# Moving the work region and the two halves of x inside SBUF, in a float32r transformer-layer kernel

## The chip, the cores and the metric

The kernel runs on one core of one Trainium2 chip, in a single launch. The metric is device time in microseconds (us) from one execution of the whole program; the figure for a kernel is the median of its runs. The granted TensorE clock of a stretch has two levels, 1.2 and 2.4 GHz; the profile prints them as 0.50 and 1.00, or as a mean between them.

## The reference, cut to what matters

One layer of a diffusion backbone over 512 latent tokens of width 2048, with 256 context tokens that only supply the start state of a scan. All data is float32.

```
h_lat = modulate(rms_norm(x, norm1_gain), sh1, sc1)          # 512 x 2048
h_ctx = modulate(rms_norm(ctx, norm1_gain), csh1, csc1)      # 256 x 2048
mix   = token_mixer(h_lat, h_ctx, w_in, ...)                 # w_in 2048 x 7168: gMLP heads and gated scans
x     = x + g1 * (mix @ w_out)                               # 2048 x 2048
h     = modulate(rms_norm(x, norm2_gain), sh2, sc2)
x     = x + g2 * (square(relu(h @ w_ff1)) @ w_ff2)           # 2048 x 8192, 8192 x 2048
return rms_norm(x, final_gain)
```

The shifts, scales and gates come from a further product, silu(c) @ w_ada (2048 x 12288).

## The kernel before

**Precision.** Every large product is made of three float32r products. A value is split into a high part (the float32r rounding, written by ScalarE) and a low part (the rest, by GpSimd or VectorE), and the kernel adds hi*hi, hi*lo and lo*hi in PSUM. For the latent stream the two halves of x (normalised and modulated, transposed) are `h_hi` and `h_lo`, 16 tiles of 512 columns each; for the context they are `c_hi` and `c_lo`, 16 tiles of 256 columns; for the hidden activations of the MLP they are `hid_hi` and `hid_lo`, 8 tiles of 512 columns.

**Weights.** They arrive as 448 units of 128 x 1024 through four slots `raw` (L247). ScalarE writes `w_hi` (L344), GpSimd writes `w_lo` (L313; VectorE does 32 of them in the context heads, L705), each with two slots. `lo_done` releases TensorE, `unit_used` gives the slots back.

**Two shapes of product.** A *tall* unit (lines 1105 to 1107, and 1392 to 1394 for the first units of the MLP) has 128 weight columns as the stationary operand and a tile of h (or c) as the moving operand. A *wide* unit (lines 1119 to 1121) has it the other way round: 128 columns of h, c or hid are the stationary operand, and 512 columns of weights the moving one. In the names of a matmul row, `bank<-A,B`, A is the moving and B the stationary operand; each matmul has its own weight load, listed as PEld.

**Stages, in order of time.** (1) adaLN product for the first norm: `ada1_w` is the moving operand (L1067). (2) context values, wide with c as the stationary operand, and context heads, tall with c moving. (3) latent values, half wide, half tall. (4) eight scan heads, tall with h moving, with steps of the previous head's scan between the products (L1227 and others) and the second adaLN product on VectorE (L753). (5) gMLP: u tall, v wide. (6) output projection, wide with h as the stationary operand. (7) the MLP in eight blocks: 384 tall matmuls with h moving, then 384 wide matmuls with hid as the stationary operand. Each engine runs a list written by hand, ordered by semaphores; loops over heads and blocks are hardware loops.

**Places in SBUF.** `build` hands out byte offsets within a partition. `fixed` gives the next free offset, rounded up to 32 bytes; `work` gives a place at a number of KB behind `w0`, where tensors of different stages lie over one another. The start is 16512 (the base of 16481, rounded up). So the kernel before has:

| offset (bytes) | what | offset modulo 64 |
|---|---|---|
| 16512 | raw, then w_hi (32896) and w_lo (41088) | 0 |
| 49280 to 114816 | h_hi, h_lo; in stage 1 ada1_w lies over both, and junk over h_hi | 0 |
| 114816 | ident (512 bytes) | 0 |
| 115328 | ones (32 bytes), after it mask and ten more small tensors | 0 for ones, 32 for those after it |
| 118368 to 228960 | work region of 108 KB: c_hi at +0, c_lo at +16 KB; hid_hi at +16 KB (134752), hid_lo at +32 KB (151136); x_tok, x_res, mix, scan buffers | 32 |

All tensors in the work region start at a whole number of KB behind w0, so they keep its remainder. The stationary slices are 512 bytes long and start at multiples of 512 bytes behind their tensor.

Of the kernel before, what the change touches and what calls it, by code (L numbers as in the profile page):

```python
# [28 lines left out]
F32 = mybir.dt.float32  # L29
F32R = mybir.dt.float32r  # L30
# [5 lines left out]
P = 128  # L36
D = 2048
KT = D // P
SEQ, CTX = 512, 256
# [9 lines left out]
KB = 1024  # L49
# [18 lines left out]
def build(nc, ctx_x, x, w_stream, w_ada, cols, small, masks, bs_row, final_row, ws_t, out):  # L68
    with ExitStack() as stack:
        base = nc.sbuf_base  # L70
        top = nc.sbuf_usable_end
        where = [base + (-base) % 32]

        def fixed(name, shape, dt=F32):
            n = 1 if dt == U8 else 4
            for s in shape[1:]:
                n *= s
            t = nc.alloc_sbuf_tensor_at(name, shape, dt, offset=where[0])
            where[0] += n + (-n) % 32
            return t  # L80
# [1 line left out]
        raw = fixed("raw", [P, 4, UNIT])  # L82
        w_hi = fixed("w_hi", [P, 2, UNIT], F32R)
        w_lo = fixed("w_lo", [P, 2, UNIT], F32R)
        r1 = where[0]
        h_hi = fixed("h_hi", [P, KT, SEQ], F32R)
        h_lo = fixed("h_lo", [P, KT, SEQ], F32R)
        ada1_w = nc.alloc_sbuf_tensor_at("ada1_w", [P, 4, 4096], F32, offset=r1)
        junk = nc.alloc_sbuf_tensor_at("junk", [P, D], F32, offset=r1)
        ident = fixed("ident", [P, P])  # L90
        ones = fixed("ones", [P, 8])
        mask = fixed("mask", [P, LEVELS, P], U8)
# [5 lines left out]
        oml = fixed("oml", [P, 2, HEADS])  # L98
        lbt = fixed("lbt", [P, 3, 2 * HEADS])
        stat = fixed("stat", [P, 64])  # L100
        w0 = where[0]
        assert w0 + 108 * KB <= top, (w0, top)

        def work(name, kb, shape, dt=F32):
            return nc.alloc_sbuf_tensor_at(name, shape, dt, offset=w0 + int(kb * KB))
# [6 lines left out]
        VG_COL, OG_COL = col[:, 160:168], col[:, 168:176]  # L112
        lbl = fixed("lbl", [P, 2, 2 * HEADS])
        w0 = where[0]
        assert w0 + 108 * KB <= top, (w0, top)


        c_hi = work("c_hi", 0, [P, KT, CTX], F32R)
# [1386 lines left out]
```

## Time and profile before

| | |
|---|---|
| median of 3 runs | 2747.98 us (2743.83 to 2750.40) |
| span of the profiled execution, first to last instruction | 2748.0 us |
| PE busy | 2638.0 us, 96% of the span |
| PEld, DVE, ACT, POOL busy | 2125.1, 1271.9, 728.3, 1002.8 us |
| mean granted TensorE clock | 0.984 |

The profiled execution's own time, apart from its span, is not given; the span equals the median of the runs to 0.1 us. A matmul's busy time overlaps with that of the next, so busy time doesn't say what a matmul costs. What it costs is the distance from its start to the start of the next, called its pitch here: the time of a stretch without waits divided by the number of matmuls in it.

### The profile page before, as it was taken

To read this page: it belongs to the slowest core of one execution; us is meant where nothing else is said; L and a number is where in the kernel's file an instruction comes from. 1 tells how busy PE (TensorE), PEld (TensorE's weight loads), DVE (VectorE), ACT (ScalarE), POOL (GpSimd) and SP (SyncE) were. 2 spreads that over 40 slices of the span, in tenths; PEclk is the share of its full clock that TensorE was granted. 3 is DMA by queue.
4 is the path that set the end of the run, shared out by engine and by line. 5 is a ranking of instruction groups with operands and counts; after the bars stand their busy time and mean duration, and the time that the engine had idled before them with its cause. 6 is when DMAs were issued, how large, how long until landed. Compare 5 with 4: busy or idle time off the path is not lost.

```text
span 2748.0 us, 33371 instructions
## 1 busy us (share of the span) xinstructions
PE 2638.0 (96%) x12236; PEld 2125.1 (77%) x12236; DVE 1271.9 (46%) x1495; ACT 728.3 (27%) x931; POOL 1002.8 (36%) x420
## 2 busy tenths in 40 slices
PE   8989999999999999998899999999999999999997
PEld 1469887777777887787788888888888888888885
DVE  2386447777888623666423223332332333323324
ACT  1254222222222223223322222212222122221222
POOL 0240243323332343343344444444444444444442
PEclk9999999999999999999999999999999999999998
DMA  9635454433344352364223232222222222222222
GB/s 409 250 115 166 154 193 151 146 132 122 122 137 138 131 214 92 115 232 143 69 93 114 92 99 93 98 93 95 95 92 99 92 99 92 95 96 92 99 92 99
DMA packets 104715, 353.80 MB, mean 129 GB/s; under 512 B 9937, under 2 KB 10193, under 8 KB 100689
## 3 DMA queue, kind: packets, MB, share of 16 engines
q1 hardware_dynamic: 104224, 352.46, 37.3%
q8 instruction: 40, 0.66, 0.1%
q10 hardware_dynamic: 432, 0.54, 0.1%
q14 instruction: 19, 0.15, 0.0%
HBM read 348.77 MB, written 4.19 MB: 128 GB/s over the span
## 4 chain that ended last, share of the span: by engine, by line
PE 58%; issue 28%; POOL 10%; DVE 2%; DMA 1%; ACT 1%; POOLq 0%; SPq 0%; DVEq 0%; ACTq 0%
POOL w_lo L313 10%; PE bank L1105 9%; PE bank L1107 9%; PE bank L1106 9%; PE bank L1119 9%; PE bank L1120 9%; PE bank L1121 9%; PE bank L1067 3%; DMA ada_w<-in_w_ada 1%; DVE prep_tmp L666 0%; DVE x_tok L656 0%; DVE x_res L1056 0%; ACT junk L392 0%; PE bank L1154 0%; PE bank L1092 0%
## 5 line engine op out<-in xcount | busy, mean ns | idle before, releaser
L313 POOL TENSOR_TENSOR w_lo<-raw,w_hi 128x1024 fp32r<-128x1024 f32 x416 | 1002.6, 2410 | 1719.7 <-ACT w_hi L344 1719.7
L344 ACT ACTIVATE w_hi<-raw 128x1024 fp32r<-128x1024 f32 x448 | 475.0, 1061 | 1768.6 <-PE bank L1107 870.3
L1105 PE MATMUL bank<-h_hi,w_hi 128*128 128x512 f32 x1696 | 673.3, 397 | 2.9 <-POOL w_lo L313 2.9
L1107 PE MATMUL bank<-h_hi,w_lo 128*128 128x512 f32 x1696 | 665.0, 392 | 0.0
L1106 PE MATMUL bank<-h_lo,w_hi 128*128 128x512 f32 x1696 | 664.3, 392 | 0.0
L1119 PE MATMUL bank<-w_hi,hid_hi 128*128 128x512 f32 x1024 | 404.9, 395 | 0.0
L1120 PE MATMUL bank<-w_lo,hid_hi 128*128 128x512 f32 x1024 | 404.9, 395 | 0.0
L1121 PE MATMUL bank<-w_hi,hid_lo 128*128 128x512 f32 x1024 | 404.8, 395 | 0.0
L1105 PEld LDWEIGHTS bank<-h_hi,w_hi 128*128 128x128 f32 x1696 | 321.3, 189 | 67.0 <-POOL w_lo L313 3.4
L1107 PEld LDWEIGHTS bank<-h_hi,w_lo 128*128 128x128 f32 x1696 | 320.3, 189 | 67.5
L1106 PEld LDWEIGHTS bank<-h_lo,w_hi 128*128 128x128 f32 x1696 | 321.1, 189 | 64.0
L1025 DVE TENSOR_TENSOR hid_sb<-relu_sb 128x512 f32<-128x512 f32 x64 | 159.5, 2492 | 450.2 <-ACT relu_sb L596 450.2
L753 DVE SCALAR_TENSOR_TENSOR ada_acc<-ada_w,cs,ada_acc 128x512 f32<-128x512 f32 x240 | 268.7, 1120 | 87.0 <-DMA ada_w<-in_w_ada 80.6
L1034 DVE TENSOR_TENSOR g_tmp<-bank,g_row 128x512 f32<-128x512 f32 x128 | 87.5, 684 | 476.5 <-PE bank L1121 476.5
L1121 PEld LDWEIGHTS bank<-w_hi,hid_lo 128*128 128x128 f32 x1024 | 192.1, 188 | 46.8
L1120 PEld LDWEIGHTS bank<-w_lo,hid_hi 128*128 128x128 f32 x1024 | 192.1, 188 | 46.8
L1119 PEld LDWEIGHTS bank<-w_hi,hid_hi 128*128 128x128 f32 x1024 | 192.1, 188 | 46.7
L1119 PE MATMUL bank<-w_hi,h_hi 128*128 128x512 f32 x448 | 178.5, 398 | 13.9 <-POOL w_lo L313 7.3
L1120 PE MATMUL bank<-w_lo,h_hi 128*128 128x512 f32 x448 | 176.3, 394 | 0.0
L1121 PE MATMUL bank<-w_hi,h_lo 128*128 128x512 f32 x448 | 176.3, 394 | 0.0
L1036 DVE TENSOR_TENSOR x_res<-x_res,g_tmp 128x512 f32<-128x512 f32 x128 | 153.3, 1198 | 4.4
L1119 PEld LDWEIGHTS bank<-w_hi,h_hi 128*128 128x128 f32 x448 | 85.4, 191 | 33.1 <-POOL w_lo L313 12.8
(183 smaller groups left out, 2180.9 us busy)
## 6 DMA issues: line engine op xcount, KB each, us to landing
raw<-in_w_stream SPq DMA_DIRECT2D x448, 512.0 KB, 3.5
ada_w<-in_w_ada SPq DMA_DIRECT2D x128, 512.0 KB, 4.1
ada_w<-in_w_ada SPq DMA_DIRECT2D x16, 2048.0 KB, 11.9
x_tok<-in_x SPq DMA_DIRECT2D x4, 1024.0 KB, 16.5
x_res<-in_x SPq DMA_DIRECT2D x4, 1024.0 KB, 11.9
out<-x_res SPq DMA_DIRECT2D x4, 1024.0 KB, 4.0
ctx_tok<-in_ctx_x SPq DMA_DIRECT2D x2, 1024.0 KB, 16.1
fin_row<-in_final_row SPq DMA_DIRECT2D x1, 1024.0 KB, 6.6
```

The costliest lines, as they stand in the source:

```text
L313: pool.tensor_tensor(w_lo[:, r % 2], raw[:, r], w_hi[:, r % 2].bitcast(F32), ALU.subtract).then_inc(lo_done, 1)
L344: act.activation(w_hi[:, r % 2], raw[:, r], ACT.Copy).then_inc(hi_done, 1)
L753: dve.scalar_tensor_tensor(acc[:], w[:, m % 2, t], c, acc[:], ALU.mult, ALU.add).then_inc(ada_summed, 1)
L1025: dve.tensor_tensor(hid_sb[:, t % 2], relu_sb[:, t % 2], relu_sb[:, t % 2], ALU.mult).then_inc(hid_made, 1)
L1034: dve.tensor_tensor(g_tmp[:, n % 2], bank[4 * (1 - c % 2) + t][:], g2_row[:, c * 512:(c + 1) * 512], ALU.mult).then_inc(ff2_tmp, 1)
L1036: dve.tensor_tensor(x_res[:, t, c * 512:(c + 1) * 512], x_res[:, t, c * 512:(c + 1) * 512], g_tmp[:, n % 2], ALU.add).then_inc(ff2_added, 1)
L1105: pe.matmul(dst, wh, hi[:, kt], start=(kt == 0), stop=False)
L1106: pe.matmul(dst, wh, lo[:, kt], start=False, stop=False)
L1107: mm = pe.matmul(dst, wl, hi[:, kt], start=False, stop=(kt == KT - 1))
L1119: pe.matmul(b[:], xh, wh, start=(first and k == 0), stop=False)
L1120: pe.matmul(b[:], xh, wl, start=False, stop=False)
L1121: mm = pe.matmul(b[:], xl, wh, start=False, stop=(last and k == 1))
```

## The change

`fixed` calls are put in another order. All small tensors come directly behind the weight slots; w0 follows them; the 108 KB work region follows w0; behind it come h_hi and h_lo, with ada1_w and junk again lying over them. Sizes, places within the work region, what lies over what, and every instruction's order on its engine and semaphore waits stay as they were; only start offsets are other ones. The weight slots don't move.

```diff
         w_lo = fixed("w_lo", [P, 2, UNIT], F32R)
-        r1 = where[0]
-        h_hi = fixed("h_hi", [P, KT, SEQ], F32R)
-        h_lo = fixed("h_lo", [P, KT, SEQ], F32R)
-        ada1_w = nc.alloc_sbuf_tensor_at("ada1_w", [P, 4, 4096], F32, offset=r1)
-        junk = nc.alloc_sbuf_tensor_at("junk", [P, D], F32, offset=r1)
         ident = fixed("ident", [P, P])
         ones = fixed("ones", [P, 8])
...
         lbl = fixed("lbl", [P, 2, 2 * HEADS])
         w0 = where[0]
-        assert w0 + 108 * KB <= top, (w0, top)
+        r1 = w0 + 108 * KB
+        where[0] = r1
+        h_hi = fixed("h_hi", [P, KT, SEQ], F32R)
+        h_lo = fixed("h_lo", [P, KT, SEQ], F32R)
+        ada1_w = nc.alloc_sbuf_tensor_at("ada1_w", [P, 4, 4096], F32, offset=r1)
+        junk = nc.alloc_sbuf_tensor_at("junk", [P, D], F32, offset=r1)
+        assert where[0] <= top, (where[0], top)
```

The offsets that follow:

| | before | modulo 64 | after | modulo 64 |
|---|---|---|---|---|
| small tensors | 114816 to 118368 | | 49280 to 52832 | each as before |
| work region (w0) | 118368 | 32 | 52832 | 32 |
| c_hi, c_lo | 118368, 134752 | 32 | 52832, 69216 | 32 |
| hid_hi, hid_lo | 134752, 151136 | 32 | 69216, 85600 | 32 |
| h_hi (also ada1_w), h_lo | 49280, 82048 | 0 | 163424, 196192 | 32 |

The partition has 229376 bytes (224 KB); its middle is at 114688.

## Rows read from the trace of the kernel before

**Rows 1.** Page, part 1: busy us, share of the span, instructions of each engine.
```profile
PE 2638.0 (96%) x12236; PEld 2125.1 (77%) x12236; DVE 1271.9 (46%) x1495; ACT 728.3 (27%) x931; POOL 1002.8 (36%) x420
```
**Rows 2.** Windows, busy us and instructions per stretch: output projection, then MLP tall, wide, tall.
```profile
core 0: us, PE busy (x) PEld busy (x) DVE busy (x) ACT busy (x) POOL busy (x), PEclk, DMA share, GB/s
1210.00:1240.00 30.00, 30.00 (x133) 24.82 (x134) 19.55 (x21) 8.60 (x14) 13.95 (x6) 1.00 0.81 277
1500.00:1570.00 70.00, 70.00 (x311) 57.97 (x310) 19.10 (x12) 19.93 (x25) 31.11 (x13) 1.00 0.29 93
1590.00:1660.00 70.00, 70.00 (x302) 56.29 (x301) 22.03 (x24) 13.37 (x13) 28.91 (x13) 1.00 0.30 97
1680.00:1750.00 70.00, 70.00 (x311) 57.97 (x310) 20.79 (x13) 20.97 (x26) 30.85 (x13) 1.00 0.29 97
```
**Rows 3.** One line's matmuls within 1505:1570: duration ns min/median/max, first and last start.
```profile
L1107 PE MATMUL bank<-h_hi,w_lo x96: 388/389/390, 1505.1 to 1569.7; 128*128 128x512 f32 x96
```
**Rows 4.** The same of a wide line with hid stationary, 1591:1660.
```profile
L1119 PE MATMUL bank<-w_hi,hid_hi x99: 393/396/398, 1591.3 to 1659.9; 128*128 128x512 f32 x99
```
**Rows 5.** Timeline of PE, output projection: start us, us, engine, line, operands.
```profile
1211.78 0.39 PE L1121 MATMUL bank<-w_hi,h_lo 128*128 128x512 f32 x1
1212.01 0.39 PE L1119 MATMUL bank<-w_hi,h_hi 128*128 128x512 f32 x1
...
1214.06 0.39 PE L1119 MATMUL bank<-w_hi,h_hi 128*128 128x512 f32 x1
```
**Rows 6.** Timeline of PE, context values, tiles 6 and 7 of c (ten pitches between).
```profile
129.99 0.39 PE L1120 MATMUL bank<-w_lo,c_hi 128*128 128x512 f32 x1
...
132.32 0.39 PE L1121 MATMUL bank<-w_hi,c_lo 128*128 128x512 f32 x1
```
**Rows 7.** Timeline of PE, context heads, tall with c moving, 256 columns (fifteen pitches between).
```profile
213.11 0.28 PE L1106 MATMUL bank<-c_lo,w_hi 128*128 128x256 f32 x1
...
214.88 0.29 PE L1106 MATMUL bank<-c_lo,w_hi 128*128 128x256 f32 x1
```
**Rows 8.** Groups of instructions by line: counts, busy us, mean ns.
```profile
L1106 PE MATMUL bank<-h_lo,w_hi 128*128 128x512 f32 x1696 | 664.3, 392 | 0.0
L1119 PE MATMUL bank<-w_hi,hid_hi 128*128 128x512 f32 x1024 | 404.9, 395 | 0.0
L1119 PE MATMUL bank<-w_hi,h_hi 128*128 128x512 f32 x448 | 178.5, 398 | 13.9 <-POOL w_lo L313 7.3 <-DVE h_lo L954 4.2 <-ACT mix L503 1.7
L1119 PE MATMUL bank<-w_hi,c_hi 128*128 128x512 f32 x64 | 28.1, 439 | 1.9 <-POOL w_lo L313 1.9
L1392 PE MATMUL bank<-h_hi,w_hi 128*128 128x512 f32 x32 | 14.8, 463 | 4.3 <-POOL w_lo L313 4.3
```
**Rows 9.** Writers of split halves, whole span: duration ns min/median/max, first and last start.
```profile
L668 DVE TENSOR_TENSOR h_lo<-prep_tmp,h_hi x32: 691/693/2930, 158.0 to 1320.2; 128x512 fp32r<-128x512 f32 x32
L1027 DVE TENSOR_TENSOR hid_lo<-hid_sb,hid_hi x64: 692/693/694, 1334.8 to 2645.6; 128x512 fp32r<-128x512 f32 x64
L546 ACT ACTIVATE h_hi<-mix x16: 613/616/652, 1091.5 to 1129.9; 128x512 fp32r<-128x512 f32 x16
L598 ACT ACTIVATE hid_hi<-hid_sb x64: 629/633/634, 1334.1 to 2644.9; 128x512 fp32r<-128x512 f32 x64
```
**Rows 10.** First adaLN product, and the DMA into its weights (median us to landing).
```profile
L1067 PE MATMUL bank<-ada_w,cs x224: 590/592/1058, 8.8 to 108.3; 128*2 128x512 f32 x112
ada_w<-in_w_ada SPq DMA_DIRECT2D x16, 2048.0 KB, 11.9
```
**Rows 11.** Waits: who waited for whom, us in total, times, longest; first row of 400:900.
```profile
PE bank L1227 <- DVE q_meet L803: 33.4, 22, 2.5
```

More of the change, by code:

```diff
@@ L100, in build @@
         stat = fixed("stat", [P, 64])
-        w0 = where[0]
-        assert w0 + 108 * KB <= top, (w0, top)
         def work(name, kb, shape, dt=F32):
@@ L114, in build @@
         w0 = where[0]
-        assert w0 + 108 * KB <= top, (w0, top)
+        r1 = w0 + 108 * KB
[5 more added lines that the diff above has]
+        assert where[0] <= top, (where[0], top)
         c_hi = work("c_hi", 0, [P, KT, CTX], F32R)
```

## The prediction

> **What bounds the kernel now.** I read the page's busy shares first. TensorE is busy 96% of the span [rows 1], so what counts is the cost of a matmul, not the waits of the other engines. Then the windows inside the MLP, which is half of the run. In 70 us with no wait and the clock at 1.00, 311 tall matmuls start in one window and 302 wide ones in the next, then 311 again [rows 2]. Both kinds move 512 columns over a 128-column stationary operand, with one weight load each; yet their pitch differs. Exact pitches come from one line's first and last start, since each line has every third matmul. Tall: (1569.7 - 1505.1) / (95 x 3) = 226.7 ns [rows 3]. Wide with hid stationary: (1659.9 - 1591.3) / (98 x 3) = 233.3 ns [rows 4]. The difference is 6.6 ns.
>
> It is not the wide shape. In the output projection the same lines 1119 to 1121 have h as the stationary operand, and nine matmuls take 1214.06 - 1212.01 = 2.05 us, 228 ns each to the rounding of those stamps; the window around it holds 133 in 30 us, one per 226 ns [rows 2, 5]. With the context halves stationary, ten matmuls take 132.32 - 129.99 = 2.33 us, 233 ns each [rows 6]; two in three of them have c_hi, one c_lo. So with equal weights, banks and order, h costs about 227 and hid and c cost 233. What differs is where the stationary operand lies: h starts at a multiple of 64 bytes (of 128 too) below the middle of the partition, c and hid start 32 bytes off such a multiple and above the middle.
>
> The change gives h the remainder 32 that c and hid have, and leaves theirs. It also swaps the regions: c and hid come below the middle, h above. These two readings of the 6.6 ns give different results, so I weigh them.
>
> **Remainder or place.** A slow upper part would have to begin between the last bytes of h_lo (114816) and the first of c_hi (118368), since c tiles 6 and 7 (from 124512) are already slow [rows 6]. A border at 96 or 128 KB is excluded: half the tiles of h_lo lie above 96 KB, and the output window, which uses ten tiles or more, has the fast pitch throughout [rows 2]; c_hi's tiles 6 and 7 lie below 128 KB, and with only c_lo slow the mean would be 229, not 233. Only the exact middle, 112 KB, would fit, by chance. The distance to the weights can't be it either: w_hi and w_lo are 8 KB apart and the gap between h and c is 3.5 KB. The remainder fits with no chance needed. I take it at about four to one.
>
> **Stationary or moving.** After the change h is off its multiple in both roles. Before, [rows 7] show the only float32r matmuls of before whose moving operand (c) has the remainder 32 and whose stationary operand (weights) has 0. Fifteen take 214.88 - 213.11 = 1.77 us, 118.0 ns each. The columns alone, by the 2.4 GHz level, take 256 / 2.4 = 106.7, so the rest is 11.3 ns. For 512 columns the rest is 226.7 - 213.3 = 13.4 with both operands at remainder 0 and 233.3 - 213.3 = 20.0 with the stationary one off. The rest of 11.3 is near the first, so a moving operand off its multiple seems to cost nothing. It is one case, at half the length, so the bounds of this term are 0 and 6.6 ns.
>
> **The change part by part.** No instruction is added, removed or reordered.
> - Wide matmuls with h stationary: 3 x 448 = 1344 [rows 8], in the latent values, gMLP v and the output projection. 1344 x 6.6 ns = +8.9 us. Bounds 0 and 8.9. TensorE runs through these stages; the group's whole idle time is 13.9 us, in a few waits [rows 8]. Those on GpSimd and ScalarE follow the pitch itself, since their inputs come out of the units before. I let 0.3 us be absorbed: +8.6.
> - Tall matmuls with h moving: 3 x 1696 + 3 x 32 = 5184 [rows 8]. Taken at 0; upper bound 5184 x 6.6 = +34.2 us, all in the open in the MLP, where TensorE has no wait.
> - Wide matmuls with hid or c stationary: 3 x 1024 + 3 x 64 = 3264 [rows 8]. The remainder stays, so 0; by the reading of place they get faster, lower bound -3264 x 6.6 = -21.5 us.
> - First adaLN product: ada1_w, moving, goes to remainder 32. 224 matmuls in 99.5 us [rows 10], on the path. Taken at 0; upper bound 6.6 ns, or 13.2 if each of two passes pays, 1.5 to 3.0 us. The DMA into it is 2 MB per issue and keeps its shape; I cost it at 0.
> - VectorE and ScalarE: the subtraction that writes h_lo below the middle and the one that writes hid_lo above it both have a median of 693 ns, so 0. ScalarE's copy takes 616 into h_hi and 633 into hid_hi [rows 9]; if that 17 ns is the remainder, 16 copies and the 32 of the norm are 0.8 us in all, beside TensorE's work or nearly so. I take 0.1.
> - Small tensors keep their remainders, and the weight slots don't move: 0.
>
> Sum: 2748.0 + 8.6 + 0.1 = 2756.7, so 2757. The span equals the median of the runs to 0.1 us, so nothing is added around it.
>
> The Trainium skill would say otherwise. Its page "TensorE: Matmul & The Clock Gate", section "Back-to-back issue gap", gives the isolated gap as N / 2.4 + 2.5 ns, 215.8 for 512 columns, with no term for an address; and "SBUF — State Buffer", section "Who interferes with whom", says that PE never waits on anyone. By these rules the time would stay at 2748, which is the third rival below. The trace disagrees with the first: 226.7 and 233.3, and the two differ though N is the same.
>
> **The rivals.**
> 1. *Place, not remainder, stationary only.* It ends on the other side. hid and c lose 21.5 us, h gains 8.9: 2748.0 + 8.9 - 21.5 = 2735.4. It needs a border at 112 KB; for it, that the middle does fall into the gap; against it, the coincidence. It decides in the MLP: 3072 wide matmuls at 226.7.
> 2. *The remainder costs in both roles.* 8.9 + 34.2, +2 for the first adaLN product, less what the heads hide. There TensorE waits 22 times for VectorE's q_meet [rows 11]; each wait follows some 12 tall matmuls, which would end 0.08 us later, so about 2 us are absorbed. 2748.0 + 43.1 = 2791. Against it are the context heads [rows 7]. The same with place instead of remainder in both roles gives 2791 - 21.5 = 2770.
> 3. *Nothing changes.* The offsets do what the diff says, but the 6.6 ns come from something else that c and hid share: 2748. Against it: nothing else that I find is common to the unrolled context stage and the looped MLP and absent in the output projection.
>
> **How the numbers follow.** Remainder and stationary only, 0.50: 2757, own range 2753 to 2760. Rival 1, 0.13. Rival 2 by remainder 0.15, by place 0.05. Rival 3, 0.10. Mixed cases, such as a part of the moving cost, 0.07, between 2757 and 2791. A measurement of this kernel tells 0.2%, 5.5 us, from no change. Faster is rival 1 with a little of the mixed rest, 0.13; same is rival 3 and the low edge of the first case, 0.13; slower 0.74. The range leaves out rival 1 and takes in rivals 2 and 3 with the spread of the runs, 2745 to 2792.
>
> **What the profile after would show.** Right: wide lines with h stationary at 233.3 ns, so about 129 matmuls in a 30 us window of the output projection where there were 133; 311 and 302 in the MLP windows as now. Rival 1: 309 or more in the wide MLP windows. Rival 2: 302 in the tall MLP windows, and the adaLN product longer than 99.5 us. Rival 3: the counts of now in all. A change in waits or in VectorE's times with equal pitches would make the whole argument wrong.

## The result and the profile after

The changed kernel takes 2789.01 us (median of 4 runs, 2787.8 to 2791.4), the kernel before 2747.01 us beside it. The ratio is 1.0146, with a 95% interval of 1.0133 to 1.0158: 42 us slower. The likeliest forecast was 2757 (own range 2753 to 2760); the measured time is near that of the rival "the remainder costs in both roles", 2791, which had a chance of 0.15.

The span of the profiled execution is 2786.1 us. Line numbers are one lower than before (L1106 here is L1107 of before).

Page after, part 1, as [rows 1]:

```profile
PE 2679.0 (96%) x12236; PEld 2128.3 (76%) x12236; DVE 1273.9 (46%) x1495; ACT 727.6 (26%) x931; POOL 1005.5 (36%) x420
```

All the change is on TensorE: its matmuls (PE) are busy for 41 us more, its weight loads (PEld) for 3 us more, and the other engines move by under 3 us. Windows after, in the output projection and in the MLP tall, wide, tall, as [rows 2]:

```profile
1190.00:1220.00 30.00, 30.00 (x134) 24.29 (x133) 23.24 (x24) 7.79 (x14) 12.63 (x5) 1.00 0.55 185
1520.00:1590.00 70.00, 70.00 (x301) 56.38 (x300) 19.14 (x12) 20.32 (x25) 30.67 (x13) 1.00 0.29 94
1610.00:1680.00 70.00, 70.00 (x302) 56.26 (x301) 22.00 (x24) 13.16 (x13) 31.03 (x13) 1.00 0.28 91
1700.00:1770.00 70.00, 70.00 (x302) 56.38 (x301) 19.14 (x12) 19.52 (x25) 31.24 (x13) 1.00 0.27 90
```

The tall windows fell from 311 matmuls to 301 or 302, level with the wide ones. The first window holds some short matmuls of another kind beside the wide ones, so its count says nothing; the one line within it does. Single lines after: the wide line with h stationary, the tall line as in [rows 3], and the wide line with hid as in [rows 4]:

```profile
L1118 PE MATMUL bank<-w_hi,h_hi x36: 393/396/397, 1195.3 to 1219.8; 128*128 128x512 f32 x36
L1106 PE MATMUL bank<-h_hi,w_lo x100: 394/396/397, 1520.0 to 1589.3; 128*128 128x512 f32 x100
L1118 PE MATMUL bank<-w_hi,hid_hi x99: 393/395/398, 1611.3 to 1679.9; 128*128 128x512 f32 x99
```

(1219.8 - 1195.3) / 105 = 233.3 ns, (1589.3 - 1520.0) / 297 = 233.3 and (1679.9 - 1611.3) / 294 = 233.3. Tall h went from 226.7 to 233.3, wide h too, hid stayed. Where the time went, by stages of before and after (same columns as [rows 2]):

```profile
117.70:296.90 179.20, 164.66 (x1129) 149.91 (x1128) 128.65 (x161) 85.81 (x112) 39.32 (x16) 0.96 0.40 135
296.90:1295.40 998.50, 939.67 (x4608) 785.25 (x4609) 640.35 (x854) 264.23 (x384) 349.68 (x144) 0.98 0.44 150
1295.40:1404.10 108.70, 101.25 (x462) 83.35 (x461) 47.17 (x48) 36.92 (x50) 36.12 (x15) 0.95 0.21 69
1404.10:2748.00 1343.90, 1326.27 (x5761) 1080.78 (x5759) 424.50 (x378) 326.12 (x365) 572.84 (x239) 0.99 0.29 96
```
```profile
117.40:293.00 175.60, 162.12 (x1129) 148.04 (x1128) 127.37 (x161) 85.66 (x112) 40.08 (x16) 0.97 0.42 138
293.00:1313.60 1020.60, 963.38 (x4608) 790.55 (x4608) 643.37 (x854) 263.99 (x384) 351.41 (x144) 0.97 0.44 146
1313.60:1424.40 110.80, 103.36 (x463) 83.45 (x463) 47.30 (x48) 36.93 (x50) 36.09 (x15) 0.95 0.21 68
1424.40:2786.10 1361.70, 1344.14 (x5761) 1081.04 (x5759) 424.56 (x378) 325.79 (x365) 573.07 (x239) 0.99 0.28 95
```

From the latent values to the output projection: +22.1 us. That stretch has 2112 tall and 1344 wide matmuls with h, 3456 x 6.6 = 22.8. The next stretch, the norm and the tall part of MLP block 0 (384 matmuls): +2.1. The rest: +17.8, which is the 2688 tall matmuls of blocks 1 to 7 x 6.6 = 17.7. The context stage was 3.6 us shorter in this one execution, with a clock of 0.97 instead of 0.96; this and a little at the start are why the spans differ by 38.1 and the medians by 42.0. Pitches of whole blocks below are read from the traces in the same way: 384 matmuls from the first start of one MLP part to the first start of the next.

### The profile page after: what moved, and what is told of

The parts are those of the page before. It is cut to its first block, busy times and chain, and to the rows that moved or that the text cites. A ratio compares the mean times of both kernels' runs of the same rounds, so it can differ in the third digit from the quotient of the medians.

```text
span 2786.1 us, 33371 instructions
## 1 busy us (share of the span) xinstructions
PE 2679.0 (96%) x12236; PEld 2128.3 (76%) x12236; DVE 1273.9 (46%) x1495; ACT 727.6 (26%) x931; POOL 1005.5 (36%) x420
## 4 chain that ended last, share of the span: by engine, by line
PE 58%; issue 29%; POOL 10%; DVE 1%; DMA 1%; ACT 1%; POOLq 0%; SPq 0%; DVEq 0%; ACTq 0%
POOL w_lo L312 10%; PE bank L1104 9%; PE bank L1105 9%; PE bank L1106 9%; PE bank L1118 9%; PE bank L1119 9%; PE bank L1120 9%; PE bank L1066 3%; DMA ada_w<-in_w_ada 1%; DVE prep_tmp L665 0%; DVE x_tok L655 0%; DVE x_res L1055 0%; ACT junk L391 0%; PE bank L1153 0%; PE bank L1091 0%
## 5 line engine op out<-in xcount | busy, mean ns | idle before, releaser
L1104 PE MATMUL bank<-h_hi,w_hi 128*128 128x512 f32 x1696 | 682.2, 402 | 2.9 <-POOL w_lo L312 2.9
L1105 PE MATMUL bank<-h_lo,w_hi 128*128 128x512 f32 x1696 | 673.3, 397 | 0.0
L1106 PE MATMUL bank<-h_hi,w_lo 128*128 128x512 f32 x1696 | 673.1, 397 | 0.0
L1106 PEld LDWEIGHTS bank<-h_hi,w_lo 128*128 128x128 f32 x1696 | 320.2, 189 | 77.2
```

Of the source, the lines that this page charges most:

```text
L1104: pe.matmul(dst, wh, hi[:, kt], start=(kt == 0), stop=False)
L1105: pe.matmul(dst, wh, lo[:, kt], start=False, stop=False)
L1106: mm = pe.matmul(dst, wl, hi[:, kt], start=False, stop=(kt == KT - 1))
```

## The experiments

The theory on record said: a stationary operand off a multiple of 64 bytes costs 6.6 ns, a moving one nothing. The result refuted its second half. The letters in the expectations name theories: R, the remainder of either operand costs; P, the place in the partition costs; D, the difference of the two operands' offsets costs; the others are explained where they come up. From here I write d for the difference, data tensor's offset (h, c or hid) minus weight slot's offset, modulo 512 bytes. Before: 0 for h, -32 for c and hid. After: -32 for all three.

**1. Everything at d = 0, in the changed order** (e1_after_all0). Edit, against the changed kernel:

```diff
         lbl = fixed("lbl", [P, 2, 2 * HEADS])
+        where[0] += 32
         w0 = where[0]
```

> The changed kernel with 32 bytes left free in front of the work region, so that the work region and the two halves of x behind it start at a multiple of 64 (c, hid and h at remainder 0), at the changed kernel's places. Theory R (a float32r matmul of 512 columns costs 6.6 ns more when either operand starts off a multiple of 64, wherever it lies): all pitches 226.7 ns; 9792 matmuls less 6.6 ns, so 2789 - 43 - 21.5 + 2 for the heads, about 2726 us. Theory P (place: h is slow because it lies above the middle, c and hid slow or not by remainder): tall and wide h stay at 233.3, hid goes to 226.7, so about 2767 us.

Measured: 2730.26 us (2728.75 to 2732.86), ratio to the kernel before 0.9929 (0.9913 to 0.9946). Theory R fits, P falls. The same two MLP windows now both hold 311:

```profile
1500.00:1570.00 70.00, 70.00 (x311) 57.96 (x310) 19.35 (x13) 20.49 (x25) 31.11 (x13) 1.00 0.29 97
1590.00:1660.00 70.00, 70.00 (x311) 57.95 (x310) 21.83 (x24) 13.80 (x13) 30.39 (x14) 1.00 0.30 98
```

So h above the middle of the partition is as fast as below it, and 32 bytes took 59 us off the changed kernel.

**2. h low, but off by 32** (e2_before_h32). Edit, against the kernel before:

```diff
+        where[0] += 32
         r1 = where[0]
...
         junk = nc.alloc_sbuf_tensor_at("junk", [P, D], F32, offset=r1)
+        where[0] += 32
         ident = fixed("ident", [P, P])
```

> The kernel before with 32 bytes left free in front of h_hi and 32 more in front of ident: h_hi and h_lo stay low in the partition but have remainder 32 modulo 64; the work region moves up by 64 bytes and keeps remainder 32. Theory R: h pitches 233.3 in both roles, time as the changed kernel, about 2789 us. Theory P: h stays at 226.7, 2747 us.

Measured: 2790.37 us, ratio 1.0149 (1.0132 to 1.0166). Theory R fits, P falls again. The whole slowdown comes without moving a region. Here d is +32 for h and for c and hid (their start is 64 bytes higher), where after the change it is -32; the pitch is 233.3 for both signs. Windows of tall and wide:

```profile
1520.00:1590.00 70.00, 70.00 (x302) 56.22 (x301) 21.17 (x15) 19.96 (x25) 29.01 (x13) 1.00 0.29 97
1615.00:1685.00 70.00, 70.00 (x302) 56.35 (x301) 22.00 (x24) 13.05 (x13) 29.11 (x13) 1.00 0.29 96
```

**3. The weights off as well** (e3_after_w32). Edit, against the changed kernel:

```diff
+        where[0] += 32
         w_hi = fixed("w_hi", [P, 2, UNIT], F32R)
         w_lo = fixed("w_lo", [P, 2, UNIT], F32R)
+        where[0] += 32
         ident = fixed("ident", [P, P])
```

> The changed kernel with w_hi and w_lo also moved by 32 bytes, so that weights, h, c and hid all have remainder 32 (raw, ident and the small tensors keep 0). Theory R (each operand counts by itself, the cost is paid once per matmul): 233.3 everywhere, about 2789 us. Variant R2, each operand off its multiple adds 6.6 ns: 240 ns everywhere, 9792 x 6.6 = 65 us more, about 2853 us. Theory D (what counts is the difference between the two operands' remainders): 226.7 everywhere, about 2726 us.

Measured: 2729.38 us, ratio 0.9927 (0.9911 to 0.9944). Theory D fits, and R falls. Weights, h, c and hid all lie 32 bytes off a multiple of 64, and both windows are at 311:

```profile
1500.00:1570.00 70.00, 70.00 (x311) 57.97 (x310) 19.18 (x13) 21.02 (x26) 30.51 (x14) 1.00 0.30 98
1590.00:1660.00 70.00, 70.00 (x311) 57.98 (x310) 21.85 (x24) 13.84 (x13) 31.11 (x13) 1.00 0.29 96
```

No operand's own remainder modulo 64 counts, only how the two stand to each other. (That holds for the 256-column matmuls as well: tall c has 119.9 ns here and 119.8 in experiment 1.) The small tensors and raw lie as in the changed kernel modulo 64, so they are not it.

**4. The kernel before with the work region at d = 0** (e4_before_work0, and once more as e12_before_work0_again). Edit, against the kernel before: the line of experiment 1.

> The kernel before with 32 bytes left free in front of the work region alone: c and hid at remainder 0, all places as before. Theory R: hid and wide c at 226.7 instead of 233.3, 3264 matmuls x 6.6 = 21.5 us less than before, about 2726 us. Theory P: hid stays at 233.3, 2747 us. If a 256-column matmul pays for a moving operand off its multiple, tall c falls below its 118.3 ns; if it pays nothing, as I took it in the prediction, it stays at 118.3.

> The kernel before with 32 bytes free in front of the work region, once more, beside the one with c at 192: 2729 us again, by every theory.

Measured: 2729.40 us, ratio 0.9930 (0.9913 to 0.9946), and 2730.84, 0.9934 (0.9921 to 0.9948). The loss of the kernel before on c and hid is real: 20.4 and 18.5 us against the kernel before beside each, where the working gave 21.5. It is independent of the order of the regions, since experiment 1 came out at 2730 too. Wide with c stationary fell only from a mean of 233.0 ns to 229.6, not to 226.7; on its 192 matmuls that is 0.6 us. The last sentence of the expectation is the one that bears on my error. Tall c, timeline of TensorE, columns as in [rows 7]:

```profile
213.08 0.28 PE L1106 MATMUL bank<-c_hi,w_hi 128*128 128x256 f32 x1
...
214.88 0.28 PE L1106 MATMUL bank<-c_hi,w_hi 128*128 128x256 f32 x1
```

Fifteen pitches in 1.80 us, 120.0 ns (119.8 over the stage), against 118.0 in [rows 7]. At 256 columns the case that is good for 512 is the *slower* one. Neither answer of the expectation came out: the pitch neither fell nor stayed, it rose.

**5. The loss undone with 32 bytes** (e8_after_h0). Edit, against the changed kernel:

```diff
-        r1 = w0 + 108 * KB
+        r1 = w0 + 108 * KB + 32
```

> The changed kernel with 32 bytes left free between the work region and h_hi: h gets difference d = 0 to the weights (modulo 256), everything else lies as the change puts it, c and hid at -32. Theory D (only the difference of the two operands' offsets counts): h pitches back to 226.7, hid stays 233.3, the whole loss is gone: 2747 to 2750 us, as the kernel before. If the regions' new places cost anything by themselves, it stays above.

Measured: 2749.78 us (10 runs), ratio to before 1.0003 (0.9994 to 1.0013). The regions stay where the change put them and nothing is lost; the move itself costs nothing, to 0.13%. Tall and wide hid (lines of this kernel):

```profile
L1106 PE MATMUL bank<-h_hi,w_lo x103: 389/389/389, 1500.2 to 1569.6; 128*128 128x512 f32 x103
L1118 PE MATMUL bank<-w_hi,hid_hi x101: 393/394/397, 1589.8 to 1659.8; 128*128 128x512 f32 x101
```

69.4 us / 306 = 226.8 and 70.0 / 300 = 233.3: as in the kernel before.

**6. Other differences** (e5_c64_h128, e6_c192_h256, e7_c96_h320, e10_c160_h160; one run each). Edit, against the changed kernel, with (A, B) = (96, 64), (224, 64), (128, 224), (192, 0):

```diff
         lbl = fixed("lbl", [P, 2, 2 * HEADS])
+        where[0] += A
         w0 = where[0]
...
-        r1 = w0 + 108 * KB
+        r1 = w0 + 108 * KB + B
```

> The changed kernel with c and hid moved so that they start 64 bytes, and h 128 bytes, off the weights' offset modulo 512 (in the runs so far this difference d was 0 wherever the pitch was 226.7, and +32 or -32 wherever it was 233.3). Theory D64: only d modulo 64 counts; both 226.7, about 2730 us, as with d = 0. Theory B (the two streams of TensorE meet in banks that repeat over more than 64 bytes, and d = 0 is one case of several): hid or h has a pitch other than 226.7 and 233.3, down to 213.3 + 2.5 for none at all (the 2.5 is the rest of the first adaLN product, 429.2 / 2 - 213.3 = 1.3 per pass, rounded up), or more.

> As the run with 64 and 128, with d = 192 for c and hid and 256 for h. Theory D64: both 226.7, about 2730 us. Theory B: another pitch in one of them.

> As the run with 64 and 128, with d = 96 for c and hid and 320 for h. Theory D64: hid 233.3 (96 is 32 modulo 64), h 226.7, about 2751 us. Theory B: other pitches; a 256-column matmul (tall c: 119.9 ns at d = 0, 118.3 at -32, 116.9 at +32) already tells +32 and -32 apart, which D64 can't.

> The changed kernel with c, hid and h all 160 bytes off the weights. Theory D with a period of 256 and the sign taken as stationary minus moving: tall h has moving h and so -160 = 96, which gave 234.3 as wide hid; so tall h 234.3. Wide hid and wide h have 160, not yet measured, and must agree with each other; between 226 and 235. If the sign doesn't count, tall and wide agree instead.

Measured: 2790.18, 2736.41, 2773.44 and 2792.02 us. Theory D64 (only d modulo 64 counts) falls at once: d = 64 and 128 are as slow as 32. To compare the two roles, take s = stationary minus moving, modulo 256; it is d in a wide matmul and -d in a tall one. The pitches of whole MLP blocks in ns:

| s (bytes) | 0 | 32 | 64 | 96 | 128 | 160 | 192 | 224 |
|---|---|---|---|---|---|---|---|---|
| wide hid | 226.7 | 233.3 | 233.3 | 234.3 | | 233.3 | 228.9 | 233.3 |
| tall h | 226.7 | 233.3 | | 234.3 | 233.3 | | 228.9 | 233.3 |

Three of these in single lines: tall h at s = 128 and at s = 96 (the runs with 64 and 128, and with 160), wide hid at 192:

```profile
L1105 PE MATMUL bank<-h_hi,w_hi x101: 391/397/399, 1519.8 to 1589.8; 128*128 128x512 f32 x101
L1105 PE MATMUL bank<-h_hi,w_hi x101: 392/397/400, 1519.6 to 1589.9; 128*128 128x512 f32 x101
L1119 PE MATMUL bank<-w_hi,hid_hi x102: 391/392/393, 1590.1 to 1659.5; 128*128 128x512 f32 x102
```

70.0 / 300 = 233.3 ns, 70.3 / 300 = 234.3 and 69.4 / 303 = 229.0. Two of the tall values come from other multiples: s = 0 also at d = 256, and 192 at d = 320. Where both of these roles were measured they agree, so the period is 256 bytes within what was tried, and the sign as taken. (Wide with h stationary is not in the table; at s = 128 its mean is 232.4, a little under the 233.3 of tall h.) The run with 160 foretold tall h at 234.3 and got 234.3. Zero is the best of the values tried; none reaches the 215.8 ns of the formula of the Trainium skill that the prediction cites. The two windows (tall, wide) of the run with 192 and 256, the closest:

```profile
1500.00:1570.00 70.00, 70.00 (x310) 58.02 (x310) 19.06 (x12) 20.97 (x26) 30.46 (x14) 1.00 0.29 98
1590.00:1660.00 70.00, 70.00 (x308) 57.51 (x307) 21.93 (x24) 13.79 (x13) 31.25 (x13) 1.00 0.28 97
```

The table also gives the times: for the run with 96 and 320, 2729.5 + 3072 x 7.6 ns + 1344 x 6.6 ns + 5184 x 2.2 ns = 2773.1, measured 2773.4. For the one with 160, the same sum gives 2798, measured 2792. Its MLP fits: it is 43.7 us longer than that of experiment 1, and the table gives 43.6. The missing 6 us lie before the MLP, where TensorE also waits and runs short matmuls, so pitches alone do not give that part to better than some us.

**7. Only w_lo moved** (e11_wlo32). Edit, against the changed kernel:

```diff
         w_hi = fixed("w_hi", [P, 2, UNIT], F32R)
+        where[0] += 32
         w_lo = fixed("w_lo", [P, 2, UNIT], F32R)
```

> The changed kernel with 32 bytes free between w_hi and w_lo. Small tensors, work region and h all move up by 32, so c, hid and h are at d = 0 to w_hi and at -32 to w_lo. Of each three matmuls, tall moves h_hi, h_lo, h_hi over w_hi, w_hi, w_lo; wide moves w_hi, w_lo, w_hi over h_hi, h_hi, h_lo. Theory N (what collides is a moving stream and the weight load of the NEXT matmul): in tall the pitch after the second matmul (h_lo moving, w_lo being loaded) is the long one, in wide after the second too (w_lo moving). Theory O (a matmul's own two operands): in tall it is the third, in wide the second. Both: one in three pays, mean 226.7 + 2.2 = 228.9 ns, 2729.5 + 9792 x 2.2 ns = about 2751 us. In the profile the modelled durations should show it: tall line of h_lo longer by some 6 ns under N, tall line of h_hi,w_lo longer under O.

Measured: 2786.06 us, one run; neither theory's 2751. Groups of the tall lines and of the wide lines with hid (columns as in [rows 8]):

```profile
L1105 PE MATMUL bank<-h_hi,w_hi 128*128 128x512 f32 x1696 | 680.6, 401 | 2.9 <-POOL w_lo L313 2.9
L1106 PE MATMUL bank<-h_lo,w_hi 128*128 128x512 f32 x1696 | 679.7, 401 | 0.0
L1107 PE MATMUL bank<-h_hi,w_lo 128*128 128x512 f32 x1696 | 662.9, 391 | 0.0
...
L1120 PE MATMUL bank<-w_lo,hid_hi 128*128 128x512 f32 x1024 | 409.6, 400 | 0.0
L1119 PE MATMUL bank<-w_hi,hid_hi 128*128 128x512 f32 x1024 | 404.5, 395 | 0.0
L1121 PE MATMUL bank<-w_hi,hid_lo 128*128 128x512 f32 x1024 | 402.4, 393 | 0.0
```

Within the MLP the three tall starts stand 232.5, 239.2 and 228.3 ns before their next (means of the start times), 700.0 in all, as much as three of 233.3. In order, theory N is right: the longest is the one that streams h_lo while w_lo is loaded for the next, and the matmul whose own operands differ (h_hi over w_lo) is the shortest, against O. In wide hid the pitch after the second (w_lo moving) is the longest as well: 232.5, 235.8 and 231.6. In size N is wrong: one mismatch in three costs as much as all three. And the order alone is weak support, for the three pitches are also unequal where all three pairs have the same difference. In the run with 160, wide hid has 237.1, 230.8 and 232.0 ns in the order hi over hi, lo over hi, hi over lo (groups of that run):

```profile
L1119 PE MATMUL bank<-w_hi,hid_hi 128*128 128x512 f32 x1024 | 408.5, 399 | 0.0
L1121 PE MATMUL bank<-w_hi,hid_lo 128*128 128x512 f32 x1024 | 403.4, 394 | 0.0
L1120 PE MATMUL bank<-w_lo,hid_hi 128*128 128x512 f32 x1024 | 401.4, 392 | 0.0
```

What is shown is that the 32 bytes are not a fee on each matmul whose pair is off; that they act on how the two streams fall into step is my reading, and not shown.

**8. c alone at d = 192** (e9_all0_c192). Edit, against the changed kernel:

```diff
         lbl = fixed("lbl", [P, 2, 2 * HEADS])
+        where[0] += 288
         w0 = where[0]
...
-        c_hi = work("c_hi", 0, [P, KT, CTX], F32R)
-        c_lo = work("c_lo", 16, [P, KT, CTX], F32R)
+        c_hi = work("c_hi", -0.0625, [P, KT, CTX], F32R)
+        c_lo = work("c_lo", 15.9375, [P, KT, CTX], F32R)
```

> The changed kernel's order of regions with h and hid at d = 0 and c alone at d = 192 (modulo 256), the value at which the 256-column matmuls of the context heads had 113.5 ns instead of 119.8. Theory D: 768 x 6.3 ns = 4.8 us less in the context heads, 192 x 2.2 ns = 0.4 us more in the context values, so 2729.5 - 4.4 = 2725 us, if VectorE, which makes the low parts of the weights there, keeps up; if the context heads wait for VectorE instead, 2729 us.

Measured: 2726.16 us (2723.85 to 2727.64), ratio to before 0.9922 (0.9909 to 0.9936). The version with all at zero, on the same chip beside it, took 2730.84 (2728.38 to 2732.37): the runs of the two don't overlap, though the intervals of their ratios do. Seventeen 256-column pitches take 1.93 us, 113.5 ns, in this unit of the context heads:

```profile
213.07 0.28 PE L1105 MATMUL bank<-c_hi,w_hi 128*128 128x256 f32 x1
...
215.00 0.28 PE L1107 MATMUL bank<-c_hi,w_lo 128*128 128x256 f32 x1
```

The next unit is slower, seventeen pitches in 2.00 us, 117.6 ns:

```profile
218.07 0.28 PE L1105 MATMUL bank<-c_hi,w_hi 128*128 128x256 f32 x1
...
220.07 0.28 PE L1107 MATMUL bank<-c_hi,w_lo 128*128 128x256 f32 x1
```

From here on every second unit is like this one, and the mean of the stage is 115.3 ns. In the run with 192 and 256 of experiment 6, c and the weights lie at the very same addresses, and there all units have 113.4 to 113.8. So at 256 columns the offsets alone do not fix the pitch. The context heads took 106.7 us here and 108.9 in the version with all at zero: 2.2 us, about half of the 4.8 that the expectation counted on for them.

This is the fastest kernel of the study, 21 to 23 us below the kernel before, with no instruction added or taken away.

## Why the prediction was right or wrong

- *The number.* The measured 2789 lies inside the whole range, 2745 to 2792, and slower was the likeliest direction (0.74). But it lies there only because the range also took in rival 2; the likeliest forecast missed, with +9 us where +42 were measured.
- *What bounds the kernel: right.* The pitch of float32r matmuls sets the time. A difference of 6.6 ns, on 6528 matmuls with h, explains the 42 us: 6528 x 6.6 = 43.1.
- *Remainder or place: right to refuse place.* Experiments 1, 2 and 5 have h fast and slow both below and above the middle, and hid at 233.3 after the swap. Wrong in what was put in its place: not an operand's remainder modulo 64 but the difference of the two operands modulo 256 (experiments 3 and 6). In the kernel before the weights always had the value that made the two readings the same, so its trace could not tell them apart. The prediction did raise the distance to the weights and dropped it, because w_hi and w_lo are 8 KB apart and the gap between h and c is only 3.5 KB. That excludes a distance beyond which matmuls get slower; it says nothing of a distance modulo 256, of which 8 KB is a multiple. That the same tensors get slow by either reading was luck: all weights stayed at remainder 0.
- *Wide with h stationary, +8.9: right.* 233.3 in the output projection. *Wide with hid or c, 0: right*, 233.3 in both traces for hid.
- *Tall with h moving, taken at 0, upper bound +34.2: this is the step that failed.* By the measured pitch it is 5184 x 6.6 = 34.2, its upper bound. The reason given was [rows 7]: the rest over the streaming time was 11.3 ns at 256 columns, nearer to 13.4 than to 20.0. That compared rests across two lengths, without a 256-column case at the other remainder. Experiment 4 supplied it: at d = 0 the rest is 119.8 - 106.7 = 13.1, at -32 it is 11.6. So the rest at 256 columns moves the other way, and its nearness to 13.4 told nothing about 512. The rival that priced this term, rival 2, came out with 2791.
- *What the heads absorb in rival 2, about 2 us.* Waits for q_meet went from 33.4 us [rows 11] to 32.3, both 22 times; so about 1 us less, of the 2 that were let off.
- *Nothing added around the span: not sound.* In every later run the time is 1.8 to 3.4 us above the span. So the execution with the span of 2748.0 took about 2750 (an estimate from this), and that the span met the median of the runs was chance. It is worth 2 us.
- *First adaLN product, 0: right.* Its pitch stays 429.2 ns with ada1_w as moving operand off by 32.

```profile
L1066 PE MATMUL bank<-ada_w,cs x224: 591/592/1061, 9.2 to 108.7; 128*2 128x512 f32 x112
```

- *VectorE and ScalarE: right in size, wrong in reason.* ScalarE's copy still takes 617 ns (median) into h_hi, now off by 32, and 631 into hid_hi, so the 17 ns of [rows 9] are not the remainder; what they are stays open.

The formula of the Trainium skill, "TensorE: Matmul & The Clock Gate", section "Back-to-back issue gap", N / 2.4 + 2.5 ns, has no term for an address, and is not enough for these matmuls: the same instruction list ran between 2726 and 2792 us by offsets alone. Its 2.5 ns are what is left in the first adaLN product, whose stationary operand has two columns, if each matmul that the profile lists there counts as two times 512 columns: 429.2 - 2 x 213.3 = 2.5 ns. That it does is inferred from the 429.2, not shown.

Not settled: what the two streams share. That it is a moving stream against the next weight load fits the order within the three of experiment 7, in both shapes, but the sizes there are explained by neither theory, and the run with 160 shows unequal pitches with equal pairs too. A structure of the memory with a period of 256 bytes would fit the table, but no run here shows it. Offsets off a multiple of 32 were not tried.

## What to carry to other kernels

When a kernel is bound by back-to-back matmuls, read the pitch per line (last start minus first, over the count) for each pair of operand tensors; if equal shapes give different pitches, compare the two operands' byte offsets with each other, here modulo 256, before anything else. The test is one run with a few free bytes in front of one of them. A small tensor of 32 bytes in front of a large one can set that difference, so fix the large tensors' offsets on purpose, and re-read them whenever the allocation order changes. Never carry a rest per instruction from one length to another without a pair at the second length.

## What the runs showed of the hardware

- A float32r matmul of 512 columns with a weight load of 128 columns beside it has a pitch of 226.7 ns if both operands' offsets agree modulo 256, and 228.9 to 234.3 at the seven other multiples of 32, at a granted clock of 1.00. In cycles of 2.4 GHz, worked out from these pitches, 226.7 is 544 (512 + 32) and 233.3 is 560 (512 + 48).
- At 256 columns (tall with c moving) zero is not the best: 119.8 ns at d = 0, 118.3 at -32, 116.9 at +32, and 113.5 at 192 in one run, but 113.5 and 117.8 by turns in another with the same addresses.
- At the lower level of the clock the difference is gone. After the change, with h at -32 and the clock granted at 0.50 (1.2 GHz) from 333.38 to 336.79, behind a wait of 4.6 us on TensorE:

```profile
332.79 0.79 PE L1118 MATMUL bank<-w_hi,h_hi 128*128 128x512 f32 x1 [4.57 <-POOL w_lo L312]
333.38 0.63 PE L1119 MATMUL bank<-w_lo,h_hi 128*128 128x512 f32 x1
333.81 0.63 PE L1120 MATMUL bank<-w_hi,h_lo 128*128 128x512 f32 x1
...
336.79 0.63 PE L1118 MATMUL bank<-w_hi,h_hi 128*128 128x512 f32 x1
```

Eight pitches from 333.38 on in 3.41 us are 426 ns, and 512 / 1.2 is 426.7: no rest at all. The kernel before, with h at 0 and the clock granted at 0.50 too, has the same 3.41 us for eight:

```profile
336.23 0.63 PE L1120 MATMUL bank<-w_lo,h_hi 128*128 128x512 f32 x1
...
339.64 0.63 PE L1119 MATMUL bank<-w_hi,h_hi 128*128 128x512 f32 x1
```

So in these rows the extra belongs to the fast level alone.
- With one of three pairs mismatched, the pitches in the tall MLP are 232.5, 239.2 and 228.3, and their sum is that of three mismatched ones.
